# The second mixer's input projection by split weights, in a two-block transformer kernel on one core

## The reference, cut to what matters

```python
def diff_group(q, k, v, ...):           # first block, 4 heads
    q1, q2 = q[..., :DIFF_QK], q[..., DIFF_QK:]     # DIFF_QK = 64
    k1, k2 = k[..., :DIFF_QK], k[..., DIFF_QK:]
    o1 = block_attention(q1, k1, v, bias, scale)
    o2 = block_attention(q2, k2, v, bias, scale)
    o = o1 - lam.astype(o1.dtype) * o2
...
def hybrid_mixer(xn, w_in, ret_g, hgrn_g, w_out, lb):   # second block
    proj = xn @ w_in                    # 256x1024 @ 1024x4608
    rq, rk, rv, rg, hq, hf_fwd, hf_bwd, hi, hg = jnp.split(proj, splits, axis=-1)
    q = rotary(to_heads_2(rq, RET_HEADS), pos)
    ...
    q2 = jax.nn.silu(to_heads_2(hq, HGRN_HEADS)) * (HGRN_HEAD_DIM ** -0.5)
    f = lbh + (1.0 - lbh) * jax.nn.sigmoid(z)       # z is hf_fwd or hf_bwd
    return jnp.log(f), ((1.0 - lbh) * jax.nn.sigmoid(-z)).astype(dt)
    ...
    h_out = (hgrn2_scan(q2, k_f, v2, logf_f)
             + flip_seq(hgrn2_scan(flip_seq(q2), flip_seq(k_b), flip_seq(v2), flip_seq(logf_b))))
    return jnp.concatenate([r_out, h_out], axis=-1) @ w_out
...
def expert_choice_ffn(xn, w_router, w_gate, w_up, w_down):
    gate, idx = lax.top_k(jnp.swapaxes(affinity, 1, 2), cap)
    hid = (jax.nn.silu(jnp.einsum('becd,edf->becf', xe, w_gate)) * jnp.einsum('becd,edf->becf', xe, w_up))
    ye = jnp.einsum('becf,efd->becd', hid, w_down) * gate[..., None].astype(xn.dtype)
```

## Time and profile before

| | us |
|---|---|
| median of 3 executions | 2037.74 (2037.01 to 2038.28) |
| the profiled execution | 2038.28 |
| its span, first to last instruction | 2036.3 |
| first block, both layers | 0 to 702 |
| second block, layer 1: input blocks and levels | 713 to 859 |
| second block, layer 2: input blocks and levels | 1373 to 1519 |
| last experts | 1600 to 2036 |

### The profile page before, as it was taken

The page is one execution under the profiler, slowest core; times in us unless marked ns, Lnnn a source line. Parts: engine busy times, 40 slices in busy tenths (PEclk is TensorE's granted clock), DMA queues, the critical chain, the costliest instruction groups (busy, mean ns, idle before and its releaser), DMA issues.

```text
span 2036.3 us, 25114 instructions
## 1 busy us (share of the span) xinstructions
PE 1644.7 (81%) x10420; PEld 1158.6 (57%) x10420; DVE 678.1 (33%) x1103; ACT 492.1 (24%) x861; POOL 175.4 (9%) x127
## 2 busy tenths in 40 slices
PE   7999999999999999987655656579998865565665
PEld 6899998898999888872211212128897321121211
DVE  3636666554666567330100101016723000010101
ACT  3445554353555452120000000014212000000000
POOL 0010000001000037200000000003720000000000
PEclk9999999999999999998877877889999878787878
DMA  8316555432655573358999999999336899999997
GB/s 279 104 44 228 186 187 158 128 108 71 221 186 186 193 215 104 124 241 332 421 421 421 421 421 421 421 393 286 106 122 248 346 421 421 421 421 421 421 421 306
DMA packets 197428, 559.97 MB, mean 275 GB/s; under 512 B 15240, under 2 KB 137526, under 8 KB 148934
## 3 DMA queue, kind: packets, MB, share of 16 engines
q1 hardware_dynamic: 187878, 549.93, 70.4%
q10 hardware_dynamic: 9440, 8.46, 1.3%
HBM read 557.30 MB, written 1.05 MB: 274 GB/s over the span
## 4 chain that ended last, share of the span: by engine, by line
PE 45%; issue 24%; DMA 17%; PEld 6%; DVE 5%; ACT 2%; POOL 1%; SPq 1%; PEldq 0%; ACTq 0%; DVEq 0%; POOLq 0%; another core or an unknown queue 0%
DMA ring<-in_w_down 9%; PE psum L1834 5%; PE psum L2305 5%; PE psum L1826 4%; DMA ring<-in_w_gate 3%; DMA ring<-in_w_up 3%; PE psum L2105 3%; PE psum L2029 3%; PE psum L2215 3%; PE psum L2092 2%; PE psum L2094 2%; PE psum L2093 2%; PE psum L2172 2%; PEld psum L2105 2%; PEld psum L2094 2%
## 5 line engine op out<-in xcount | busy, mean ns | idle before, releaser
L2305 PE MATMUL psum<-ring,arena 128*32 128x512 f32 x2960 | 477.4, 796 | 318.8 <-DMA ring<-in_w_up 127.2
L2305 PEld LDWEIGHTS psum<-ring,arena 128*32 128x32 f32 x2960 | 113.7, 141 | 657.0 <-issue 654.3
L784 DVE TENSOR_TENSOR W<-ring,W 128x2048 fp32r<-128x2048 f32 x88 | 199.8, 2272 | 137.3 <-ACT W L779 137.1
L2092 PE MATMUL psum<-XT,W 128*128 128x256 f32 x704 | 199.9, 284 | 0.1
L2094 PE MATMUL psum<-XT,W 128*128 128x256 f32 x704 | 199.2, 283 | 0.0
L2093 PE MATMUL psum<-XT,W 128*128 128x256 f32 x704 | 199.1, 283 | 0.0
L779 ACT ACTIVATE W<-ring 128x2048 fp32r<-128x2048 f32 x88 | 164.6, 1893 | 80.5 <-PE psum L2094 58.1
L1778 DVE TENSOR_TENSOR arena<-arena,psum 128x512 f32<-128x512 f32 x16 | 11.0, 690 | 476.2 <-PE psum L2305 476.2
L1826 PE MATMUL psum<-XT,ring 128*128 128x256 f32 x640 | 139.4, 379 | 0.0
L2092 PEld LDWEIGHTS psum<-XT,W 128*128 128x128 f32 x704 | 133.9, 190 | 1.3 <-DVE XT L750 0.5
L2093 PEld LDWEIGHTS psum<-XT,W 128*128 128x128 f32 x704 | 133.9, 190 | 0.8
(11 more groups left out here) (270 smaller groups left out, 2273.2 us busy)
## 6 DMA issues: line engine op xcount, KB each, us to landing
ring<-in_w_up SPq DMA_DIRECT2D x170, 1024.0 KB, 17.6
ring<-in_w_down SPq DMA_DIRECT2D x142, 1024.0 KB, 18.9
ring<-in_w_gate SPq DMA_DIRECT2D x116, 1024.0 KB, 18.4
ring<-in_w_in SPq DMA_DIRECT2D x56, 1024.0 KB, 8.7
arena<-in_w_gate SPq DMA_DIRECT2D x12, 1024.0 KB, 11.9
ring<-in_w_o SPq DMA_DIRECT2D x8, 1024.0 KB, 5.6
ring<-in_w_out SPq DMA_DIRECT2D x8, 1024.0 KB, 5.1
ring<-in_w_down SPq DMA_DIRECT2D x16, 512.0 KB, 14.2
```

The source lines that it names most:

```text
L784: nc.vector.tensor_tensor(W2[split_pair(v)][:, 0:n], slot(v % SLOTS_1, n), W1[split_pair(v)][:, 0:n].bitcast(F32), ALU.subtract).then_inc( ...
L2092: nc.tensor.matmul(dst, w1[:, k, c], XT1[:, k, :], start=(k == 0), stop=False)
L2305: last = nc.tensor.matmul(psum[CAP * e:CAP * (e + 1), bank + c, :], src[:, 2 * pair + k, CAP * e:CAP * (e + 1)], tiles[e][:, k, 512 * c:51 ...
```

## The change

Three things are changed.

- The 18 input blocks of the second mixer are made as three single-pass products of split operands, 48 matmuls for a block instead of 16. ScalarE writes each block's first part (`split_round_2`), GpSimd the second part of ten blocks in two halves each (0, 2, 3, 5 to 10; `split_rest_by_pool`; block 0 included), and VectorE that of the others (1, 4, 11 to 17; `split_rest_2`). The rows are split too. Three pairs of split tiles, the split rows and five raw slots share the ring; seven slots of the split tiles go back to the experts behind the last level.
- Forget blocks alternate with queries: zf0, rq0, zf1, rq1, zb0, hq0, zb1, hq1, and so on. Ten blocks stand ahead of the levels, one in front of each of the first eight, none behind. The queries' and gates' silu is taken later, over whole tiles (`queries`, `gates`).
- In the differential attention `scores([j, j + 1])` makes both units of a head in the even step, the two units' matmuls side by side.

The second unit's scores have gone to the step ahead, beside the first unit's. The diff, cut to its core:

```diff
-IN2_BLOCKS = [("zf0", 2560), ("zf1", 2816), ("zb0", 3072), ("zb1", 3328), ("hq0", 2048), ("hq1", 2304),
-              ("rq0", 0), ("rq1", 256), ("rk0", 512), ("rk1", 768), ("rv0", 1024), ("rv1", 1280),
+IN2_BLOCKS = [("zf0", 2560), ("rq0", 0), ("zf1", 2816), ("rq1", 256), ("zb0", 3072), ("hq0", 2048), ("zb1", 3328),
+              ("hq1", 2304), ("rk0", 512), ("rk1", 768), ("rv0", 1024), ("rv1", 1280),
               ("hi0", 3584), ("hi1", 3840), ("rg0", 1536), ("rg1", 1792), ("hg0", 4096), ("hg1", 4352)]
+N_IN2 = len(IN2_BLOCKS)
+FORGET_AT = [i for i, (name, _) in enumerate(IN2_BLOCKS) if name[0] == "z"]
...
-ITEMS = ([("in", i) for i in range(10)]
-         + [("rot", 0), ("in", 10), ("rot", 1), ("in", 11), ("rot", 2), ("in", 12), ("rot", 3)]
-         + [("in", i) for i in range(13, 18)] + [("score", h) for h in range(HEADS)])
+BEFORE_LEVELS = 10
+ITEMS = [("in", i) for i in range(BEFORE_LEVELS)]
+for level in range(LEVELS):
+    if 4 <= level < 8:
+        ITEMS.append(("rot", level - 4))
+    if BEFORE_LEVELS + level < N_IN2:
+        ITEMS.append(("in", BEFORE_LEVELS + level))
+ITEMS += [("score", h) for h in range(HEADS)]
...
+RAW_2 = [[0, 1, 2, 3, 4], [9, 10, 11, 3, 5]]
+FIRST_2 = [[6, 7, 5], [4, 1, 6]]
+SECOND_2 = [[8, 9], [0, 2]]
+ROWS_2 = [[10, 11], [7, 8]]
+REST_BY_DVE = [1, 4] + list(range(11, N_IN2))
+REST_BY_POOL = [v for v in range(N_IN2) if v not in REST_BY_DVE]
+def raw_slot(lay, use):
+    return RAW_2[lay][use % len(RAW_2[lay])]
+def split_homes(lay):
+    return sorted(FIRST_2[lay] + SECOND_2[lay] + ROWS_2[lay])
...
         return None, EXTRA_AT.index(n)
-    return ring_slot(lay, MIXER_USES + n - sum(x < n for x in EXTRA_AT)), None
+    order = [raw_slot(lay, N_IN2 - 1)] + split_homes(lay) + [raw_slot(lay, N_IN2 + i) for i in range(4)]
+    return order[(n - sum(x < n for x in EXTRA_AT)) % SLOTS], None
...
+        def split_round_2(act, lay, v):
+            past = before(DEPTH + lay)
+            s = raw_slot(lay, v)
+            act.wait_ge(slot_loaded[s], 16)
+            act.sem_clear(slot_loaded[s])
+            if v >= 3:
+                act.wait_ge(proj2, past(proj2) + ITEM_AT["in", v - 3] + 1)
+            elif lay:
+                claim_for_split(act, [FIRST_2[lay][v]] + SECOND_2[lay][v:v + 1])
+            elif v == 0:
+                act.wait_ge(up_mm, past(up_mm))
+            else:
+                act.wait_ge(down_mm, past(down_mm) + v - 2)
+                if v == 2:
+                    claim_for_split(act, FIRST_2[lay][2:])
+            nc.scalar.activation(W1_2[lay][v % 3][:, :], slot(s), ACT.Copy).then_inc(rounded, 1)
+        def split_rest_2(dve, lay, v):
+            past = before(DEPTH + lay)
+            dve.wait_ge(rounded, past(rounded) + v + 1)
+            nc.vector.tensor_tensor(W2_2[lay][v % 3][:, :], slot(raw_slot(lay, v)), W1_2[lay][v % 3][:, :].bitcast(F32),
+                                    ALU.subtract).then_inc(rest, 1)
+        def split_rest_by_pool(pool, lay, v, halves=(0, 1)):
+            past = before(DEPTH + lay)
+            pool.wait_ge(rounded, past(rounded) + v + 1)
+            for i in halves:
+                c = slice(SLOT_W // 2 * i, SLOT_W // 2 * (i + 1))
+                pool.tensor_tensor(W2_2[lay][v % 3][:, c], slot(raw_slot(lay, v))[:, c], W1_2[lay][v % 3][:, c].bitcast(F32),
+                                   ALU.subtract).then_inc(rest_pool, 1)
         block = ctx.enter_context(nc.Block())
...
             pool.wait_ge(fin_rms, 1)
             pool.tensor_tensor(rs, rs, expo[:, 0:TT], ALU.pow).then_inc(fin_rms, 1)
             for lay in range(DEPTH):
                 past = before(DEPTH + lay)
+                if lay:
+                    split_rest_by_pool(pool, lay, 0, (0,))
                 norm_pool(pool, past, 0)
...
+                split_rest_by_pool(pool, lay, 2)
+                split_rest_by_pool(pool, lay, 3)
+                deep(0)
+                split_rest_by_pool(pool, lay, 5)
+                deep(1)
+                split_rest_by_pool(pool, lay, 6)
+                split_rest_by_pool(pool, lay, 7)
+                deep(2)
+                split_rest_by_pool(pool, lay, 8)
+                split_rest_by_pool(pool, lay, 9)
+                deep(3)
+                split_rest_by_pool(pool, lay, 10)
...
+                def queries():
+                    act.wait_ge(emp_act, past(emp_act) + emptied_by(ITEM_AT["in", 7])[1])
+                    nc.scalar.activation(hqT, hqT, ACT.Silu).then_inc(silus, 1)
+                    act.wait_ge(silus, past(silus) + 1)
+                    nc.scalar.activation(hqT, hqT, ACT.Copy, scale=HD ** -0.5).then_inc(silus, 1)
...
                 nc.scalar.preload_act_table_set(EXP_LN_SET)
-                for n in range(4):
-                    empty(n)
-                    if n:
-                        key_inverse_and_log(n - 1)
-                key_inverse_and_log(3)
-                for n in range(4, 6):
-                    empty(n)
+                for i in range(9):
+                    empty(i)
+                    split_round_2(act, lay, i + 3)
+                    if i in (1, 3, 5, 6):
+                        key_inverse_and_log((1, 3, 5, 6).index(i))
+                    if i == 7:
+                        queries()
                 level_exp(0)
...
+                    empty(8 + l)
+                    if 11 + l < N_IN2:
+                        split_round_2(act, lay, 11 + l)
...
+                for i in range(8 + len(HALVES), N_IN2):
+                    empty(i)
+                gates()
...
-                    if b:
+                    if b == 0:
+                        split_rest_2(dve, lay, 4)
+                    else:
                         keys_and_sums(b - 1)
...
                     if 5 <= it < 9:
                         rotate(it - 5)
+                    if 11 + it < N_IN2:
+                        split_rest_2(dve, lay, 11 + it)
...
+            def columns_of(out, w, xt, c0, m, ready=None):
+                w1, w2 = w
+                xt1, xt2 = xt
                 for k in range(KD):
-                    if fresh is not None:
-                        wait_turned(pe, past, fresh, k)
-                    last = nc.tensor.matmul(out, wt[:, k, c0:c0 + m], XT[:, k, :], start=(k == 0), stop=(k == KD - 1))
+                    c = slice(c0, c0 + m)
+                    if ready:
+                        ready(k)
+                    nc.tensor.matmul(out, w1[:, k, c], xt1[:, k, :], start=(k == 0), stop=False)
+                    nc.tensor.matmul(out, w1[:, k, c], xt2[:, k, :], start=False, stop=False)
+                    last = nc.tensor.matmul(out, w2[:, k, c], xt1[:, k, :], start=False, stop=(k == KD - 1))
...
+                    qk = [unit_operands(j) for j in js]
                     for t, (a, b) in enumerate(((0, P), (P, SPAN))):
-                        dst = psum[:, j % 2, a:b]
-                        last = nc.tensor.matmul(dst, q[:, t * P:(t + 1) * P], k[:, 0:b - a], start=True, stop=True)
-                    last.then_inc(scored, 1)
+                        for j, (q, k) in zip(js, qk):
+                            last = nc.tensor.matmul(psum[:, j % 2, a:b], q[:, t * P:(t + 1) * P], k[:, 0:b - a],
+                                                    start=True, stop=True)
+                            if t:
+                                last.then_inc(scored, 1)
...
                 def step(j):
-                    if j < NU:
-                        scores(j)
+                    if j < 2 * DIFF_H:
+                        if j % 2 == 0:
+                            scores([j, j + 1])
+                    elif j < NU:
+                        scores([j])
...
+                def split_ready_2(v):
+                    if v in REST_BY_DVE:
+                        pe.wait_ge(rest, past(rest) + REST_BY_DVE.index(v) + 1)
+                    elif v:
+                        pe.wait_ge(rest_pool, past(rest_pool) + 2 * REST_BY_POOL.index(v) + 2)
+                    else:
+                        return
+                    pe.sem_inc(slot_free[raw_slot(lay, v)], 1)
+                def rows_and_rest_ready(k):
+                    pe.wait_ge(xt_rest, past(xt_rest) + k + 1)
+                    if k % (KD // 2) == 0:
+                        pe.wait_ge(rest_pool, past(rest_pool) + 2 * k // KD + 1)
+                    if k == KD // 2:
+                        pe.sem_inc(slot_free[raw_slot(lay, 0)], 1)
...
-                        wt = wait_slot(ring_slot(lay, i)).rearrange("p (k n) -> p k n", k=8)
+                        split_ready_2(i)
+                        wt = by_row_blocks([t[lay][i % 3] for t in (W1_2, W2_2)])
...
-                for n in range(6):
+                for n in range(BEFORE_LEVELS):
                     item(n)
                 for l in range(LEVELS):
                     if 4 <= l < 8:
                         item(ITEM_AT["rot", l - 4])
-                    item(ITEM_AT["in", 6 + l])
```

(7 more changed lines are left out.)

208 lines of the change are left out of this document (110 added, 98 removed).

## The result

The changed kernel is slower: 2067.38 us (median of 4, 2063.72 to 2068.43) against 2037.38 beside it; ratio 1.0141, 95% interval 1.0129 to 1.0154. The forecast was 2030 with a range up to 2047. The profiled execution's span is 2065.7 us, 29.4 more than before. In the table, as in the rest, times are in us, the first product is TensorE's first matmul of block 0, and level 0 begins with its scores.

A forecast was written before the change was run, and what follows sets the result against it. Experts were taken as transfer-bound, so mixer time reaches the end; GpSimd and VectorE hold each other off there. Mixer 1.4 + 75 + 64 + 4 = 144.4 against 146.25; 2038.28 - 3.8 - 4 = 2030.5, median 2030, range 2006 to 2047.

The forecast's parts named there:

- GpSimd and VectorE exclude each other: In the mixer, only one of the two can hold a time, a whole instruction at a time.
- The second rival: In the levels, VectorE's second part gets ahead of GpSimd's second key product; 8 us more a layer, 2046 in all; chance 0.25.
- Level 0: Start of the mixer's first level, taken as 75 us behind the first input block.
- my own sum of what both hold: Up to level 0's keys: GpSimd 38.0 and VectorE 31.3, together 69.3, begun 4.5 us in; level 0 at 73.8 or later.
- the walk through both lists: Going through GpSimd's and VectorE's instructions in turn up to level 0 gave 76.4 us; 75 was taken.
- The levels: Seven level steps at 8.75 us, 61.3, plus 2.7 for second parts beside rotations and 4 for the last scores.
- would run while TensorE makes the scores: In the levels, VectorE's second part (2.2 us) stands behind its merge and was expected to run during TensorE's scores.
- The start: Splitting the rows ahead of the mixer's first block makes its start 1.4 us later.
- The products: In the mixer's input blocks, 48 split products take 5.76 us a block instead of 6.91.
- The map scores: In the differential attention, a head's two units side by side save between 0 and 5.2 us; 4 taken.
- The experts: The expert stage, bound by its transfers, stays as long as before; seven returned slots need 17 us of transfers.
- The good end: Every second part ready before its block: mixer 132.7 us, 13.6 less in each layer; as a rival, 2006.5, chance 0.22.

The follow-up runs named there:

- the one wait: Changed kernel, with VectorE's second part in six turns of the levels begun only when GpSimd has finished both key products of that level; 2047.99 us.
- The best kernel: Changed kernel with every second part by VectorE, in the levels behind GpSimd's keys, two orders changed, rotations moved to levels 6, 6, 7, 7; 2019.2 us.

## Where the prediction was right and wrong

- **The direction was wrong; the cause was on the page.** The forecast held that GpSimd and VectorE exclude each other, and still had the mixer 1.9 us under before in each layer. It came 15 over. The second rival in full had 2046; the result is 21 us above that, since level 0 came late as well and the levels cost more than the rival's 8.
- **Level 0: a term too small.** I counted 1.8 us that a half holds, from the earlier trace rows; the rows above show 2.14 to 2.2. In my own sum of what both hold (69.3 and 4.5), sixteen halves of 0.4 more make 80.2. Level 0 came 80.2 and 80.6 us behind the first product, not 75: 5.4 us a layer. That the sum meets it so closely is in part luck. It was meant as a lower bound, it counts 0.9 for each of four clamps, and the one shown above held VectorE for less, and the walk through both lists (76.4) with the same 6.4 more would give 82.8. The walk had the right form, and I then took less than it said.
- **The levels: the rival was the case.** I gave 61.3 + 2.7 + 4 = 68 and priced the second part getting ahead of the second key product at 8 us a layer with a quarter's chance. The failed step is "would run while TensorE makes the scores". It gets ahead by 0.01 us (1475.85 and 1475.86); the levels took 81.1, 13.1 more than forecast, and the one wait took 9.7 of them away again. The earlier trace rows had a tie, 0.09 us between the merge's end and the key product's start, and I took it as won because it was won there. It was lost in all three turns in which the second part stands right behind a merge, in both layers (key pairs of 5.7 to 5.8 us, levels 1 to 3). The first two turns have no merge; in the second of them GpSimd was ahead and the second part was held (3.36 us for 2.28). In the last two a rotation stands between.
- **Left out: TensorE's clock.** In the earlier trace rows it was 1.00 all through, and my sum had nothing for it. Once TensorE waits, the scores of a level take up to 3.8 us instead of 2.05, on the chain, where GpSimd waits for them. Layer 2's rows separate the two: the three key pairs take 17.1 us instead of 10.7, 6.4 more, and the scores of levels 0 to 6 take 19.8 instead of 13.9, 5.9 more. With the wait the scores of levels 1 to 4 are at 2.05 again, those of level 0 are not.
- **The start: mis-sized.** 1.4 us a layer; layer 2's first product came 5.0 later behind the scores than before. The copy and the norm, held for 2 us each, are most of it; without second parts on GpSimd, in seven kernels, the start came 1.1 to 3.0 later.
- **The second parts on GpSimd are nine**, not ten as I wrote; the sum up to level 0 has the right eight.
- **The products: right.** Blocks come every 5.76 us where their operands are there.
- **The map scores: right, a little small.** 4, with 5.2 as the bound; 6.0 alone. The bound came from the plain product's rate, and a unit's own record of 0.92 would have given 7.4. The Trainium skill (TensorEngine Tiling (Array Packing), Theoretical Speedup) has up to twice for 64 rows, and the pair's 0.93 for one unit's 0.92 agrees.
- **The experts: right.** Scores to the end 517.9 against 517.3, with DMA at 0.99 and 408 GB/s in the 21 us behind the scores, where it was 0.02: the seven slots arrive there.
- **The good end** (132.7 a layer) was not reached. The best kernel has 137.4 and 137.6, which is 8.6 under the kernel before in each layer. The gain is real, and two things lost it: the helper, and an order of two instructions that nothing fixed.

## What to carry to other kernels

Before work is moved to GpSimd to relieve VectorE, add what both hold in SBUF as if they were one engine, with each small dependent VectorE instruction paying a whole GpSimd one; here VectorE did 18 us more work and was busy for 12 us less. Where two engines take turns at margins of 0.1 us, don't take the order as given: here the unfixed order lost in every turn where it was a tie, and a wait that fixes it had no cost that the runs show. When a wait is found in front of an engine, ask who is late on the chain: the 8.5 us on ScalarE cost nothing, and 2.1 us in each of three key pairs a layer, with what they did to the scores behind them, cost 19.4.

## What the runs showed of the hardware

- A GpSimd subtraction of 128x1024 float32 from SBUF into fp32r held a VectorE instruction behind it for 2.1 to 2.2 us, one of 128x512 for 0.5 to 1.1, whatever the size of the held one: a copy of 28 columns went from 0.18 to 2.13 us.
- VectorE instructions with one SBUF input were held as well (the copy, and the norm's tensor_scalar, 5.05 us for two instead of 0.88); its merge out of PSUM was not (1.28 us beside a key product, 1.27 before).
- GpSimd's clamp, a tensor_scalar of 128x512 and 2.1 us, hardly held VectorE: 1.22 us for two instructions of 0.87 together, and 0.69 for one of 0.69.
- Two matmuls on 64 rows each, on the two halves of the array, took 0.93 us where one took 0.92.
- Scores of a level took 3.79 us at a granted clock of 0.50, behind 7.7 us with TensorE nearly idle, and 2.05 at 1.00.
